# WKV recurrence of an RWKV-7 block: the 64-token inverse built whole, one step ahead, in place of being applied in two halves

## The reference

```python
def _wkv7_scan(r, w, k, v, kk, a):
    # S_t = S_{t-1} diag(w_t) - (S_{t-1} kk_t) (a_t*kk_t)^T + v_t k_t^T ; y_t = S_t r_t
    def step(S, inp):
        r_t, w_t, k_t, v_t, kk_t, a_t = inp
        sa = jnp.einsum('bhvk,bhk->bhv', S, kk_t)
        S = (S * w_t[:, :, None, :]
             - sa[..., None] * (kk_t * a_t)[:, :, None, :]
             + v_t[..., None] * k_t[:, :, None, :])
        y = jnp.einsum('bhvk,bhk->bhv', S, r_t)
        return S, y
    ...
    _, ys = lax.scan(step, S0, xs)
    return jnp.moveaxis(ys, 0, 1)
```

## Time and profile before

| | |
|---|---|
| median of 3 runs | 2265.32 us (2265.12 to 2267.7) |
| the profiled execution's own time | 2263.27 us |
| its span | 2261.5 us |
| PE busy | 2159.9 us (96%) |
| DVE busy | 1493.1 us (66%) |
| ACT busy | 1076.2 us (48%) |
| granted TensorE clock, mean | 0.984 of full speed |

### The profile page before, as it was taken

One profiled execution on the slowest core, in us unless ns is written; L12 is line 12 of the kernel. 1 busy time (PEld: TensorE's weight loads), 2 busy tenths in 40 slices (PEclk: granted clock), 3 DMA queues, 4 the chain that ended last, 5 costly groups with the idle time before them and its releaser, 6 DMA issues.

```text
span 2261.5 us, 40007 instructions
## 1 busy us (share of the span) xinstructions
PE 2159.9 (96%) x15520; PEld 1852.3 (82%) x15520; DVE 1493.1 (66%) x2040; ACT 1076.2 (48%) x1506; POOL 92.2 (4%) x77
## 2 busy tenths in 40 slices
PE   7999989999999999999799999997799999999997
PEld 6888868888888888888588878887688888888886
DVE  6666558885578856885874589763476644567655
ACT  5444555444444434445544755433343644456543
POOL 0700000000000000000000000001210000000000
PEclk9999989999999999999899999999999999999998
DMA  8655445655665556656365555652354455654552
GB/s 275 203 167 158 160 132 179 190 186 186 190 190 186 188 187 190 186 167 196 121 217 143 172 161 164 208 155 65 90 166 159 158 183 195 187 148 145 167 183 89
DMA packets 402744, 384.06 MB, mean 170 GB/s; under 512 B 43505, under 2 KB 401137, under 8 KB 401777
## 3 DMA queue, kind: packets, MB, share of 16 engines
q1 hardware_dynamic: 402610, 382.18, 54.4%
HBM read 374.78 MB, written 7.34 MB: 169 GB/s over the span
## 4 chain that ended last, share of the span: by engine, by line
PE 87%; DVE 8%; issue 2%; ACT 2%; DMA 1%; SPq 0%; DVEq 0%; POOL 0%; ACTq 0%
PE acc L763 45%; PE acc L766 22%; PE acc L787 3%; PE aux L1098 2%; PE acc L842 2%; PE acc L844 2%; PE acc L843 2%; PE acc L790 2%; DVE w_lo L1930 2%; PE acc L1098 1%; ACT w_hi L1329 1%; PE aux L1254 1%; PE aux L1013 1%; PE aux L1033 1%; DVE inverse L2359 0%
## 5 line engine op out<-in xcount | busy, mean ns | idle before, releaser
L1930 DVE TENSOR_TENSOR w_lo<-raw_w,w_hi 128x1024 fp32r<-128x1024 f32 (+1 forms) x592 | 715.5, 1229 | 464.1 <-ACT w_hi L1329 463.1
L1329 ACT ACTIVATE w_hi<-raw_w 128x1024 fp32r<-128x1024 f32 (+1 forms) x592 | 612.7, 1046 | 684.3 <-PE acc L766 573.7
L763 PE MATMUL acc<-h,w_hi 128*128 128x512 f32 x1664 | 525.9, 397 | 1.2 <-DVE w_lo L1930 1.2
L766 PEld LDWEIGHTS acc<-h,w_lo 128*128 128x128 f32 x1664 | 312.6, 188 | 73.8
L766 PE MATMUL acc<-h,w_lo 128*128 128x256 f32 x1664 | 327.1, 278 | 0.0
L763 PEld LDWEIGHTS acc<-h,w_hi 128*128 128x128 f32 x1664 | 254.6, 189 | 2.2 <-issue 1.4
L763 PE MATMUL acc<-x_split,w_hi 128*128 128x512 f32 x704 | 225.2, 401 | 0.0
L763 PE MATMUL acc<-ff,w_hi 128*128 128x512 f32 x704 | 221.6, 396 | 2.4 <-DVE ff L2175 2.4
L763 PE MATMUL acc<-xs_b,w_hi 128*128 128x512 f32 x512 | 162.5, 399 | 1.7 <-DVE w_lo L2368 0.9
L766 PEld LDWEIGHTS acc<-ff,w_lo 128*128 128x128 f32 x704 | 132.2, 188 | 31.2
L766 PEld LDWEIGHTS acc<-x_split,w_lo 128*128 128x128 f32 x704 | 132.2, 188 | 31.2
(11 more groups left out here) (355 smaller groups left out, 3136.9 us busy)
## 6 DMA issues: line engine op xcount, KB each, us to landing
raw_w<-in_w_up SPq DMA_DIRECT2D x176, 512.0 KB, 3.6
raw_w<-in_a_w_in SPq DMA_DIRECT2D x128, 512.0 KB, 3.4
raw_w<-in_w_in SPq DMA_DIRECT2D x64, 512.0 KB, 3.9
raw_w<-in_w_down SPq DMA_DIRECT2D x64, 512.0 KB, 3.3
raw_w<-in_b_w_qg SPq DMA_DIRECT2D x64, 512.0 KB, 3.8
raw_w<-in_w_o SPq DMA_DIRECT2D x32, 512.0 KB, 3.3
raw_w<-in_a_w_out SPq DMA_DIRECT2D x32, 512.0 KB, 3.4
raw_w<-in_w_k_shared SPq DMA_DIRECT2D x32, 512.0 KB, 3.3
```

Of the source, the lines that this page charges most:

```text
L763: pe.matmul(ACC[2 * b + f], WHI[:, q, k, f * P:(f + 1) * P], op[:, kt, :, :].rearrange("p h t -> p (h t)"), start=first, stop=False)
L766: mm = pe.matmul(ACC[2 * b + f][:, 0:T], WLO[:, slot, k, f * P:(f + 1) * P], op[:, kt, 0, :], start=False, stop=last)
L1329: act.activation(WHI[:, u % 4, 0:ku, :], RAWW[:, u, 0:ku, :], ACT.Copy).then_inc(hi_made, 1)
L1930: dve.tensor_tensor(WLO[:, u, 0:ku, :], RAWW[:, u, 0:ku, :], WHI[:, u % 4, 0:ku, :].bitcast(F32), ALU.subtract)\
```

## The change

The whole 64 x 64 inverse is made before its step needs it. With T turned (`inverse_turned`, a product with the identity), the three products are: that turning, C T (`cross_by_inverse`), to which DVE adds the identity (`cross_and_one`), and T (C T + 1) = M (`full_inverse`). ACT copies M into place `FULL` of `SMALL` (`full_ready`), and a step's u is then one product of M with x and one copy. In step n PE turns T of step n + 2 and makes C T and M of step n + 1. Before step 0 the same is done for steps 0 and 1.

With it go other moves. `turns(n + 1)` stands right behind the product for u. The update of `S` is made in `XU_BANKS` right behind the copy of u, ahead of the products of y. `group_squares` stands behind that, and PE waits right behind it until DVE has read the sums. ACT copies M at the end of a step, once y is done. DVE does `cross_and_one` and a copy of the turned T ahead of `read_pairs`. SP starts `load_t(n)` when M of step n - 3 is copied, instead of when y of step n - 3 is done. The order of SP's transfers is the same.

The diff, cut to its core:

```diff
@@ SP
             for n in range(3, 4 * NCH):
-                sp.wait_ge(y_done, n - 2)
+                sp.wait_ge(full_ready, n - 2)
                 load_t(n)
@@ PE
+            def blocks_in(n):
+                pe.wait_ge(t_loaded[n % 3], 96 * (n // 3 + 1))
+            def inverse_turned(banks, col, n, start, stop):
...
+                blocks_in(n)
+                return quads(banks, col, CHUNK, block_of(TB[:, n % 3, :, :]), one, True, True, start, stop)
+            def cross_by_inverse(banks, col, n, stop):
+                return quads(banks, col, CHUNK, block_of(CRS[:, n % 3, :, :]), tok(small(0, INVERSE)), True, True, True, stop)
+            def full_inverse(n, start, stop):
+                return quads(Y_BANKS, T, CHUNK, tok(CROSS_ONE), block_of(TB[:, n % 3, :, :]), True, True, start, stop)
...
             def step(n):
...
                 if c > 0:
                     x_second(n)
                 if more:
+                    pe.wait_ge(tok_out, 2 * n + 2)
+                    mm = cross_by_inverse(TOK_BANKS, 0, n + 1, not two_more)
+                    if two_more:
+                        mm = inverse_turned(TOK_BANKS, P, n + 2, False, True)
+                    mm.then_inc(w_done, 1)
                     pairs(n + 1)
-                pe.wait_ge(t_loaded[n % 3], 96 * (n // 3 + 1))
+                pe.wait_ge(full_ready, n + 1)
                 pe.wait_ge(xs_ready, n + 1)
-                quads(XU_BANKS, P, CHUNK, inverse, tok(XS), True, True, True, True).then_inc(u_done, 1)
+                quads(XU_BANKS, P, CHUNK, block_of(small(m, FULL)), tok(XS), True, True, True, True).then_inc(u_done, 1)
+                if more:
+                    turns(n + 1)
+                pe.wait_ge(us_ready, n + 1)
+                if c < 3:
+                    quads(XU_BANKS, T, CHUNK, tok_kind(m, K_TOK), tok_kind(m, V_TOK), True, False, True, False)
+                    quads(XU_BANKS, T, CHUNK, tok_kind(m, BET_TOK), tok(US), True, False, False, True).then_inc(s_done, 1)
                 if n:
                     pe.wait_ge(y_out, n)
-                if c > 0:
-                    quads(Y_BANKS, 0, CHUNK, state, at(R, n), False, False, True, False).then_inc(s_read, 1)
-                pe.wait_ge(us_ready, 2 * n + 1)
-                quads(XU_BANKS, T, CHUNK, cross, tok(US), True, True, True, True).then_inc(w_done, 1)
                 if c == 0 and g:
                     group_squares(g - 1)
-                if more:
-                    turns(n + 1)
-                pe.wait_ge(ws_ready, n + 1)
-                quads(XU_BANKS, P, CHUNK, inverse, tok(XS), True, True, True, True).then_inc(u_done, 1)
...
+                    pe.wait_ge(gn_read, g)
+                if c > 0:
+                    mm = quads(Y_BANKS, 0, CHUNK, state, at(R, n), False, False, True, False)
+                if more:
+                    mm = full_inverse(n + 1, c == 0, False)
+                mm.then_inc(s_read, 1)
                 pe.wait_ge(rest_out, n + 1)
+                pe.wait_ge(s_read, n + 1)
...
@@ ACT
-                act.wait_ge(u_done, 2 * n + 2)
-                act.activation(in_slots(US), by_two(XU_BANKS[:, :, P:T]), ACT.Copy).then_inc(us_ready, 1)
                 if c == 1 and g:
                     head_rstd(g - 1)
...
                     tok_copies(n + 1)
+                    act.wait_ge(y_done, n + 1)
...
+                    act.activation(inverse4, by_two(Y_BANKS[:, :, T:384]), ACT.Copy).then_inc(full_ready, 1)
@@ DVE
                 if more:
+                    dve.wait_ge(w_done, n + 5)
+                    cross_and_one(TOK_BANKS[:, :, 0:P])
+                    if n + 2 < len(STEPS):
+                        inverse_out(TOK_BANKS[:, :, P:T])
...
-                dve.wait_ge(w_done, n + 1)
-                dve.tensor_tensor(slots(XS), by_two(XU_BANKS[:, :, T:384]), slots(XS), ALU.add).then_inc(ws_ready, 1)
```

More of the change, by code:

```diff
@@ L261, in program @@
                     GCE = sb(s3, "chunk_decay", [P, KD, NCH])
-                    INVR = sb(s3, "kk_inverse_rows", [P, T])
+                    with ExitStack() as s4:
+                        INVR = sb(s4, "kk_inverse_rows", [P, T])
+                    CROSS_ONE = sb(s3, "cross_by_inverse_and_one", [P, 4, CHUNK])
             with ExitStack() as s2:
@@ L449, in program @@
         g_dram, b_dram = dram("head_rstd_scratch", (3, P, T)), dram("bonus_scratch", (P, T))
-        AKK, ARK, ARB = range(3)
+        AKK, ARK, ARB, FULL, INVERSE = 0, 1, 2, 3, 7
         def small(m, n):
@@ L1134, in pairs, with ones_through, one @@
                     pe.wait_ge(rest_out, n)
[L1135 to L1137 removed]
                 quads(PAIR_BANKS, 0, P, at(K, n), rho_kappa, False, True, True, False)
                 quads(PAIR_BANKS, T, CHUNK, at(BET, n), at(R, n), False, True, False, True).then_inc(prep_done, 1)
+            def ones_through(n):
+                return 3 + 2 * n - (n == len(STEPS) - 1)
+            def blocks_in(n):
+                pe.wait_ge(t_loaded[n % 3], 96 * (n // 3 + 1))
+            def inverse_turned(banks, col, n, start, stop):
+                def one(h_, i):
+                    q = h_ ^ i % 2
+                    return IDENT[64 * q:64 * q + 64, 64 * q:64 * q + 64]
+                blocks_in(n)
[4 more added lines that the diff above has]
+                return quads(Y_BANKS, T, CHUNK, tok(CROSS_ONE), block_of(TB[:, n % 3, :, :]), True, True, start, stop)
             def turns(n):
@@ L1194, in step @@
                 m = n % 2
-                more = n + 1 < len(STEPS)
-                inverse, cross = block_of(TB[:, n % 3, :, :]), block_of(CRS[:, n % 3, :, :])
+                more, two_more = n + 1 < len(STEPS), n + 2 < len(STEPS)
                 if c > 0:
@@ L1216, in step @@
-                pe.wait_ge(tok_out, 2 * n + 2)
-                if c < 3:
-                    pe.wait_ge(rest_out, n + 2)
-                    quads(PAIR_BANKS, 384, CHUNK, tok_kind(m, K_TOK), tok_kind(m, V_TOK), True, False, True, False)
-                if c == 0 and g:
-                    pe.wait_ge(gn_read, g)
+                    mm = full_inverse(n + 1, c == 0, False)
+                mm.then_inc(s_read, 1)
                 pe.wait_ge(rest_out, n + 1)
-                quads(Y_BANKS, 0, CHUNK, tok_kind(m, V_TOK), tok(small(m, ARK)), True, False, c == 0, False)
@@ L1224, in step @@
-                pe.wait_ge(us_ready, 2 * n + 2)
-                if c < 3:
-                    quads(PAIR_BANKS, 384, CHUNK, tok_kind(m, BET_TOK), tok(US), True, False, False, True).then_inc(s_done, 1)
+                pe.wait_ge(s_read, n + 1)
+                quads(Y_BANKS, 0, CHUNK, tok_kind(m, V_TOK), tok(small(m, ARK)), True, False, False, False)
+                quads(Y_BANKS, 0, CHUNK, tok(US), tok(small(m, ARB)), True, False, False, True).then_inc(y_done, 1)
                 if more:
+                    if c < 3:
+                        pe.wait_ge(s_taken, 3 * g + c + 1)
@@ L1228, in step @@
                     x_first(n + 1)
-                quads(Y_BANKS, 0, CHUNK, tok(US), tok(small(m, ARB)), True, False, False, True).then_inc(y_done, 1)
+            inverse_turned(XU_BANKS, T, 0, True, True).then_inc(w_done, 1)
+            inverse_turned(TOK_BANKS, P, 1, True, True).then_inc(w_done, 1)
             pairs(0)
+            pe.wait_ge(cross_one, 1)
+            cross_by_inverse(XU_BANKS, T, 0, True).then_inc(w_done, 1)
+            pe.wait_ge(cross_one, 2)
+            full_inverse(0, True, True).then_inc(w_done, 1)
@@ L1768, in step @@
                     head_rstd(g - 1)
-                if n + 1 < len(STEPS):
+                if n == len(STEPS) - 1:
+                    operand_hi(0)
+                else:
                     tok_copies(n + 1)
+                    act.wait_ge(y_done, n + 1)
+                    inverse4 = small((n + 1) % 2, FULL).rearrange("p (j e) t -> p e j t", e=2)
+                    act.activation(inverse4, by_two(Y_BANKS[:, :, T:384]), ACT.Copy).then_inc(full_ready, 1)
                 if n in SPLIT_AT:
@@ L2474, in head_pair, with cross_and_one, inverse_out @@
                 ins.then_inc(gn_out, 1)
-            dve.wait_ge(t_stored, 16)
+            by_slots = lambda x: x.rearrange("p (e j) t -> p e j t", e=2)
+            def cross_and_one(banks):
+                one = STACK.unsqueeze(1).unsqueeze(1).broadcast_to([P, 2, 2, CHUNK])
+                dve.tensor_tensor(by_slots(CROSS_ONE[:, :, :]), by_two(banks), one, ALU.add).then_inc(cross_one, 1)
+            def inverse_out(banks):
+                dve.tensor_copy(by_slots(small(0, INVERSE)), by_two(banks)).then_inc(cross_one, 1)
+            dve.wait_ge(t_stored, 16)
+            dve.wait_ge(w_done, 1)
+            inverse_out(XU_BANKS[:, :, T:384])
+            dve.wait_ge(w_done, 3)
+            cross_and_one(XU_BANKS[:, :, T:384])
+            inverse_out(TOK_BANKS[:, :, P:T])
+            dve.wait_ge(w_done, 4)
```

(1 more changed line is left out.)

31 lines of the change are left out of this document (13 added, 18 removed).

## The result

Twelve runs of the changed kernel have a median of 2276.11 us (2271.58 to 2285.66), twelve of the kernel before, run beside them, 2266.03 us (2263.96 to 2271.45). The ratio is 1.0046, with a 95% interval from 1.0035 to 1.0058: **10.1 us slower**, where +15.4 had been forecast. The profiled execution took 2281.81 us, 5.7 above the median, so what its trace shows of loss is more than 10.1 us: its span is 18.2 us longer than that of the earlier trace rows. 11.3 of these lie in the stage.

The account below looks back on a forecast made before the run. PE was taken to run out of code once per 256-instruction block, 3.9 us each whatever the work. Terms 7.6 - 1.8 + 8.6 + 1.0 = +15.4 us on 2265.32 gave 2280.7, forecast 2280, range 2268 to 2291.

Parts of the forecast that it names:

- The blocks, asked for two steps earlier: Steps 6 and 10: PE waits 7.5 us each for T and C behind `spread_rows`; less what they cover, +8.6 us.
- Rival (1): Steps 6 and 10: blocks arrive in time, only the code counts; 2272 us, chance 0.11.
- More products: Product calls 224 to 240: 499 more instructions, 1.95 blocks of code at 3.89 us each, +7.6 us.
- wrong if ordinary blocks take under 3.5: Sign against the forecast: ordinary 256-instruction blocks under 3.5 us would mean the chain or the work did count.
- The shorter chain: From x to u: gives time back only in the last step, -1.8 us (bounds -2.9 and 0).
- Rival (4): Changed stage: "issue" pauses are really the chain from x to S, so the shorter chain wins; 2253 us, chance 0.05.
- rival (3): Changed stage: no floor per block; ACT waits go, execution and the waits for blocks count; 2273 us, chance 0.11.
- The clock: Behind long pauses PE runs at 0.60 of its clock for some 3.7 us, as it did before; nothing added.
- Group norm: PE waits for DVE's sums at c = 0, and for the update of `S` in steps 8 and 12: +1.0 us.
- Ordinary steps: Other steps: `load_t(n)` takes 6 to 7 us of a 7.8 us step, hidden by about 1 us; nothing added.
- rival (2): Ordinary loads are late too, some 10 steps waiting 1 us each; 2290 us, chance 0.11.
- Before step 0: Four more products and three DVE operations ahead of the first u, already in the product count; nothing more added.

Follow-up runs that it names:

- before_shift_128: Kernel before with four idle products (128 instructions) put ahead of step 0: 2266.68 us, ratio 1.0007 to the kernel before.
- roots_in_halves: Changed kernel with blocks ahead of roots, `a_w_out` units moved, x read back after the last y, and roots read back in two halves: 2266.72 us, ratio 1.0009.
- spread_later_no_turning: Changed kernel with roots issued behind the next step's blocks, and no turned inverse block made in the steps: 2262.36 us, ratio 0.9990 to the kernel before.
- spread_later: Changed kernel with the roots' store and reading back issued behind the next step's blocks (blocks first): 2267.36 us, ratio 1.0012 to the kernel before.
- the shifts: Two or four idle products ahead of step 0: in the kernel before, ratios 0.9998 and 1.0007; in the changed kernel with blocks first, 1.0032 and 1.0044.

## Why the prediction was right, and where it wasn't

The sign was right, and so was the mechanism of the largest term. The range held the time, and the sum was 5 us too high. The terms behind it were right to different degrees, and one was left out.

- **The blocks, asked for two steps earlier (+8.6, 0 to 18): right, and shown.** Two waits of 8.24 and 6.97 us stand where two of 7.5 had been put; with the blocks first they go, and the time falls by 7.7 us (some 4 either way). The parts hold too: the store 5.1 us behind x (5.0), the rest 11.5 (10.6), and a cover that came back as pauses of 3.42, 2.45 and 3.88 us once the waits were gone. Rival (1), blocks in time, is excluded by the same rows.
- **More products (+7.6, 0 to 8.2): too large here; this is the term that was off.** "Each block costs 3.9 us whatever PE does in it" was read from six blocks in one trace, and two of the six were picked to show that the work has no part. Of all six the shortest has the least work and the longest nearly the most. Sixteen products more cost 3.9 us (1.4 to 6.3), and the blocks of that kernel took 3.54 us. All of the change but the waits for blocks comes to +2.7 us (-0.2 to +5.7), where 7.6 - 1.8 + 1.0 = 6.8 had been summed up. The two figures fit each other: 3.9 - 2.2 + a part of the 2.6 below. As a mean the 3.9 us isn't refuted: over both sides a block came to 4.6 us, and 3.9 is the median distance of two packets of code. What fails is its use as the price of the next two blocks. That the blocks of the changed kernel took 3.82 to 4.62 us, near the forecast's 3.9, proved nothing: "wrong if ordinary blocks take under 3.5" looked at the wrong kernel.
- **The shorter chain (-1.8): right in size, in part by luck.** The end of the stage gives 2.2 in the profiled executions and 1.2 at full clock. The 2.9 us between the two copies of u were read at a clock of 0.69; at full clock they are 2.37 us apart (`before_shift_128`), and 2.37 - 0.92 - 0.2 is the 1.2 found. Inside the steps the waits for ACT fell from 6.9 to 1.3 us, and with the code held equal only 2.3 us came back in all. Rival (4) is out by the packets too: each pause named "issue" ends behind one. Half of rival (3) holds, since there is no fixed floor. That the named waits come back as time, its other half, shows nowhere, though no run has the short chain without its costs.
- **The clock (nothing added): a term left out.** Behind each of the two waits PE worked for about 4.9 us at 1.2 GHz, behind the pauses of before in the same steps for 3.4. `roots_in_halves`, with the same 3888 matmuls in the stage and a clock of 0.99, has PE busy for 98.7 us; the changed kernel for 101.5 at 0.92. An estimate from these: some 3 of the 5.0 us more of busy time are the clock. With the blocks first it is no better (0.93, 102.6), so the clock is hardly in the 7.7 us above.
- **Group norm (+1.0, 0 to 4).** Three waits for the sums, 1.6 us, and two for `wkv_s` in steps 8 and 12, 1.0 us: 2.6, at the places named and within the bounds. Two waits for `wkv_s` in other steps, 0.6 us, are gone for it, so 2.0 net. No run takes them away alone.
- **Ordinary steps (0): right.** The two waits are the only ones for blocks; rival (2) is excluded. The margin is as small as said, though: in `spread_later_no_turning`, where the blocks go first and the steps are shorter, waits of 1.53 and 1.77 us for them are left.
- **Before step 0 (0): too low in the profiled execution.** The first copy of x comes 2.6 us later. The products in it were in the count, so part of this belongs to the first term; what the chain adds beside them wasn't tried.
- **Step 14** was in no step. It is 4.5 us shorter in the profiled execution, since its pauses of before aren't there. That looks like chance and not like the change: of the twelve other traces (without the 512 waits) nine have a pause of 2.2 to 3.9 us within 5 us ahead of the last copy of x, `spread_later` the longest.

The Trainium skill's 128 KB for TensorE ("Advanced Engine Details and Errata", "ISA Cache") had spoken for rival (3). In rows, the changed kernel still stops every 126 to 128 matmuls, which speaks for few lines of 256 instructions. The kernel with one product less goes from 1529.80 to 1544.30 with 504 weight loads and no pause named "issue", but four packets came in that time too, 3.4 to 3.7 us apart. So the code of the next block can be there before PE needs it, and no trace shows it further ahead than that. No run here shows how many lines there are.

**What stays open.** What sets the length of a block, 3.3 to 4.6 us in these traces. PE's execution alone doesn't (2.69 us of work took 3.34, and 3.33 took 4.62), nor does a fixed time to bring the code. The packets narrow it down: from the start of a packet to PE going on it is 2.2 to 3.3 us, and what varies most is how long after the beginning of a block the packet starts. It is still 1.0 to 2.1 us where less than 60 GB/s of data are under way and PE waits for nothing in between (127 pauses, median 1.2), and no run shows why. Why taking a product away gives three to four times what adding one costs (twice, by the stages in the traces) is part of the same question, and so are the shifts. Leaving out the short waits of PE for its own products (1.6 us), which the change adds, wasn't tried.

## What to carry to other kernels

When a wait for loaded data moves earlier, look at what the issuing queue has to do before that load: here a wait for ACT's root, and its way out to DRAM and back, stood in front of them. That order on SP did no harm as long as the blocks were due two steps later, and then it put 15 us of waits on PE. A wait covers the pauses near it, so removing it gives back less than its length (15.2 us of waits gave 7.7). And a cost per block of code read from one trace of pauses is to be tested by one added and one removed product before it carries a sum: it was half as large on one side and nearly twice on the other, and near 3.9 us only as a mean of both. A piece of time read behind a long pause is to be held against the clock of its window, too: 2.9 us at 0.69 were 2.4 at full speed.

## What the runs showed of the hardware that was not expected

- Waiting instructions on PE whose condition holds already stood 106 ns apart in rows of 32, and left PE idle for 96 ns each (49.0 us over 512). A whole product of 32 instructions takes 0.40 us (3.19 us for eight in the earlier trace rows), so four such waits cost one product. Their rows also brought the clock of the stage to 0.81, which made the same matmuls 16.8 us longer.
- One packet of code of 16.4 KB per block of 256 instructions, no two less than 3.3 us apart in thirteen traces, each at least 1.0 us behind the pause before it, and PE going on 2.2 to 3.3 us behind its start. In a long pause the packet starts late; it is not slower once it has started.
- Pauses for code vanish where PE stands for another reason: no entry "issue" of another kind in the run with the 512 waits, and 8.2 us less of it in the changed kernel.
- A product less per step (16 in all) gave 11 to 18 us, a product more cost 1.4 to 6.3, with the same 512 instructions.
- The long pauses, 2.5 to 3.9 us, stand behind 512 KB of reading back; with 256 KB at a time they were 1.2 to 1.8 us in two of three places, but more of them, at no gain in the time.
